# A transformer/SSD block on one core: the first 16 conditioning sums move from VectorE to TensorE

## What is computed

```python
mod = jax.nn.silu(c) @ w_ada[l] + b_ada[l]           # conditioning: 6 vectors of 1024
mod_c = jax.nn.silu(c_ctx) @ w_ada[l] + b_ada[l]     # the same for the context tokens
sh1, sc1, g1, sh2, sc2, g2 = jnp.split(mod, 6)
y, yc = hybrid_mixer(x * (1 + sc1) + sh1, ctx * (1 + csc1) + csh1, w_in[l], ..., w_out[l])
x = layer_norm(DEEPNORM_ALPHA * x + g1 * y, ln1_g[l], ln1_b[l])
x = layer_norm(DEEPNORM_ALPHA * x + g2 * swiglu(x * (1 + sc2) + sh2, ...), ln2_g[l], ln2_b[l])
```

## Time and profile before

| | |
|---|---|
| median of 3 runs | 3288.69 us (3285.17 to 3290.09) |
| profiled execution, its own time | 3289.66 us |
| its span, first to last instruction | 3287.8 us |
| mean granted TensorE clock | 0.977 |
| PE busy | 3098.7 us, 94% |
| DVE busy | 2165.9 us, 66% |
| ACT busy | 1181.9 us, 36% |
| POOL busy | 1482.7 us, 45% |
| DMA | 280.13 MB, mean 85 GB/s |

### The profile page before, as it was taken

One profiled execution on the slowest core, in us unless ns is written; L12 is line 12 of the kernel. 1 busy time (PEld: TensorE's weight loads), 2 busy tenths in 40 slices (PEclk: granted clock), 3 DMA queues, 4 the chain that ended last, 5 costly groups with the idle time before them and its releaser, 6 DMA issues. The chain is left out here.

```text
span 3287.8 us, 43629 instructions
## 1 busy us (share of the span) xinstructions
PE 3098.7 (94%) x16570; PEld 2628.7 (80%) x16570; DVE 2165.9 (66%) x3294; ACT 1181.9 (36%) x2273; POOL 1482.7 (45%) x1151
## 2 busy tenths in 40 slices
PE   4999989899999999999998999989899999999997
PEld 3798878788778888888886789878787778887886
DVE  8758977685676566635667467946776575555556
ACT  5267742361433222221113347732443322322113
POOL 0544222354434445446555464213454454555665
PEclk9999999999999999999999999999999999999999
DMA  8200042003122433425331200031022122224331
GB/s 329 97 1 1 1 144 73 15 27 128 58 77 75 148 124 124 138 86 205 125 114 45 90 1 1 1 129 33 17 87 83 66 102 77 77 94 156 97 96 64
DMA packets 96175, 280.13 MB, mean 85 GB/s; under 512 B 8416, under 2 KB 21856, under 8 KB 94560
## 3 DMA queue, kind: packets, MB, share of 16 engines
q1 hardware_dynamic: 91264, 257.42, 22.8%
q10 hardware_dynamic: 4704, 19.92, 1.5%
HBM read 224.89 MB, written 52.43 MB: 84 GB/s over the span
## 5 line engine op out<-in xcount | busy, mean ns | idle before, releaser
L3976 DVE SCALAR_TENSOR_TENSOR x_res<-ps,mod,x_res 128x512 f32<-128x512 f32 (+1 forms) x448 | 308.2, 689 | 234.8 <-PE ps L214 234.0
L3381 POOL TENSOR_TENSOR h_a_lo<-f_wraw,h_a_hi 128x512 fp32r<-128x512 f32 x126 | 183.1, 1469 | 390.7 <-ACT h_a_hi L3376 390.7
L212 PE MATMUL ps<-f_ahi,f_whi 128*128 128x512 f32 (+1 forms) x896 | 341.4, 381 | 11.2 <-DVE x_res L3976 8.4
L214 PE MATMUL ps<-f_ahi,f_wlo 128*128 128x512 f32 (+1 forms) x896 | 328.1, 366 | 0.0
L213 PE MATMUL ps<-f_alo,f_whi 128*128 128x512 f32 (+1 forms) x896 | 327.9, 366 | 0.0
L213 PE MATMUL ps<-h_lo,h_a_hi 128*128 128x512 f32 (+1 forms) x720 | 249.8, 347 | 0.0
L212 PE MATMUL ps<-h_hi,whic 128*128 128x512 f32 (+1 forms) x544 | 199.0, 366 | 15.0 <-DVE wloc L464 15.0
L212 PEld LDWEIGHTS ps<-f_ahi,f_whi 128*128 128x128 f32 x896 | 169.8, 189 | 51.7 <-DVE x_res L3976 12.3
L3732 POOL TENSOR_TENSOR f_alo<-f_gated,f_ahi 128x512 fp32r<-128x512 f32 (+1 forms) x95 | 120.1, 1281 | 180.6 <-ACT f_ahi L3922 180.5
L213 PE MATMUL ps<-h_lo,whic 128*128 128x512 f32 (+1 forms) x544 | 197.0, 362 | 0.0
L214 PE MATMUL ps<-h_hi,wloc 128*128 128x512 f32 (+1 forms) x544 | 196.7, 362 | 0.0
(11 more groups left out here) (395 smaller groups left out, 8988.1 us busy)
## 6 DMA issues: line engine op xcount, KB each, us to landing
f_wraw<-in_w_ffn SPq DMA_DIRECT2D x130, 512.0 KB, 4.5
ada_w<-in_w_ada SPq DMA_DIRECT2D x56, 512.0 KB, 6.0
h_hi_f<-in_w_ada SPq DMA_DIRECT2D x56, 512.0 KB, 4.0
o_wraw<-in_w_out SPq DMA_DIRECT2D x28, 512.0 KB, 3.6
act_spill<-f_gated SPq DMA_DIRECT2D x20, 640.0 KB, 3.3
wrawc<-in_w_in SPq DMA_DIRECT2D x24, 512.0 KB, 4.2
f_gated<-act_spill SPq DMA_DIRECT2D x19, 640.0 KB, 5.2
x_spill<-x_res ACTq DMA_DIRECT2D x16, 640.0 KB, 5.6
```

The lines of the kernel that those rows point to most:

```text
L212: pe.matmul(out, w_hi, h_hi, start=first, stop=False)
L214: return pe.matmul(out, w_lo, h_hi, start=False, stop=last)
L3381: pool.tensor_tensor(self.flat(self.lo[f]), src, raw(self.flat(self.hi[f])), ALU.subtract) \
L3976: dve.scalar_tensor_tensor(out=x, in0=pl.bank(down_bank(i) + d % 2, tn), scalar=pl.mod[:, G2 + n, who:who + 1], in1=x, op0=ALU.mult, op1=A ...
```

## The change

In the opening of layer 0 the sixteen sums are made on PE. Both condition vectors come as 16 columns (`cond_columns`, 8 KB), ACT applies Silu to them, and `tensor` multiplies each of a tile's eight 128x128 weight blocks with two columns, summed in PSUM bank 6 or 7. The weights come in that block layout (`w_first`, same size). The sums of tiles 0 and 1 stand ahead of all products in PE's queue, those of k+2 behind the products of tile k. DVE adds the bias straight from PSUM. The row-shaped conditions, still wanted for the 16 later sums, are loaded behind the last `x` tile and their Silu stands at the end of ACT's loop. Both ring blocks are loaded after `x` tile 0; DVE splits them at k = 1 in place of k = 2. The scaling by ALPHA and the stores are gone; `project_out` of layer 0 loads the input again from `xT`, and ACT scales it in five instructions, with a new count (`x_scaled`) for which DVE waits. The core of the diff:

```diff
@@ -355,34 +355,47 @@
+    columns = pl.small[:, 16:32]
+    columns_in, columns_ready = pl.sem("open_columns_in"), pl.sem("open_columns_ready")
...
     def sync(sp, ring_loads):
-        ada.start(sp)
+        sp.dma_start(columns, a["cond_columns"]).then_inc(columns_in, 16)
+        sp.sem_inc(ada.tile_done, ada.SLOTS)
+        sp.sem_inc(ada.first_done, 2 * KT)
         for n, tile in enumerate(order):
             s = n % ada.SLOTS
             sp.wait_ge(ada.tile_done, n + 1)
-            sp.dma_start(ada.w[s][:, :], a["w_ada"][0, tile]).then_inc(ada.w_in[s], 16)
+            sp.dma_start(ada.w[s][:, :], a["w_first"][tile]).then_inc(ada.w_in[s], 16)
+            if n == 0:
+                sp.dma_start(pl.bada[:, :], a["b_ada"][0]).then_inc(ada.bias_in, 16)
             if n % 2 == 1:
                 k = n // 2
                 sp.dma_start(pl.x[:, k, :], a["xT"][:, k, :]).then_inc(x_in[k], 16)
-                if k < 2:
-                    ring_loads[k]()
+                if k == 0:
+                    ring_loads[0]()
+                    ring_loads[1]()
+        sp.dma_start(ada.cond[:, :, :], a["cond"]).then_inc(ada.cond_in, 16)
         sp.dma_start(pl.const[:, :], a["consts"]).then_inc(consts_in, 16)
 
+    def tensor(pe, k):
+        if k == 0:
+            pe.wait_ge(columns_ready, 1)
+        if k >= 2:
+            pe.wait_ge(biased, k - 1)
+        sums = pl.bank(6 + k % 2, 4)
+        for j in range(2):
+            n = 2 * k + j
+            w = ada.w[n % ada.SLOTS]
+            pe.wait_ge(ada.w_in[n % ada.SLOTS], 16 * (n // ada.SLOTS + 1))
+            for i in range(KT):
+                mm = pe.matmul(sums[:, 2 * j:2 * j + 2], w[:, i * P:(i + 1) * P], columns[:, 2 * i:2 * i + 2],
+                               start=(i == 0), stop=(i == KT - 1))
+            mm.then_inc(ada.tile_done, 1)
+
     def vector(dve, between):
-        def product(n):
-            s, tile = n % ada.SLOTS, order[n]
-            dve.wait_ge(ada.w_in[s], 16 * (n // ada.SLOTS + 1))
-            dve.wait_ge(ada.tile_done, n + ada.SLOTS)
-            for c, done in ((0, ada.first_done), (1, ada.tile_done)):
-                dve.scalar_tensor_tensor(out=ada.product[:, :], in0=ada.w[s][:, :], scalar=1.0,
-                                         in1=ada.cond[:, c, :], op0=ALU.mult, op1=ALU.mult,
-                                         accum_out=pl.mod[:, tile, c:c + 1]).then_inc(done, 1)
-                if c == 0:
-                    dve.wait_ge(done, n + 1)
-
         def rest_of(k):
             dve.wait_ge(rounded, k + 1)
             dve.tensor_tensor(pl.lo[:, k, :], tmp[k % 3][:, :], raw(pl.hi[:, k, :]), ALU.subtract) \
...
-        dve.wait_ge(ada.cond_ready, 1)
         for k in range(KT):
-            product(2 * k)
-            product(2 * k + 1)
             dve.wait_ge(ada.tile_done, 2 * k + 2 + ada.SLOTS)
             part = pl.mod[:, SH1 + k:SC1 + k + 1:KT, :]
             bias = pl.bada[:, SH1 + k:SC1 + k + 1:KT].unsqueeze(2).broadcast_to([P, 2, 2])
-            dve.tensor_tensor(part, part, bias, ALU.add).then_inc(biased, 1)
+            sums = pl.bank(6 + k % 2, 4).rearrange("p (t c) -> p t c", c=2)
+            dve.tensor_tensor(part, sums, bias, ALU.add).then_inc(biased, 1)
             if k >= 1:
                 rest_of(k - 1)
-            if k == 2:
+            if k == 1:
                 between()
         rest_of(KT - 1)
         dve.wait_ge(consts_in, 16)
 
     def scalar(act, between):
-        ada.silu(act)
+        act.wait_ge(columns_in, 16)
+        act.activation(columns, columns, ACT.Silu).then_inc(columns_ready, 1)
         for k in range(KT):
             act.wait_ge(biased, k + 1)
             act.wait_ge(x_in[k], 16)
...
             act.activation(pl.hi[:, k, :], tmp[k % 3][:, :], ACT.Copy).then_inc(rounded, 1)
-            act.activation(pl.x[:, k, :], pl.x[:, k, :], ACT.Copy, scale=ALPHA).then_inc(kept, 1)
-            act.wait_ge(kept, k + 1)
-            act.dma_start(pl.x_dram[:, k, :], pl.x[:, k, :]).then_inc(spilled, 16)
             if k == 0:
                 between()
-        act.wait_ge(spilled, KT * 16)
-
-    return Lead({c: [(rest, KT)] for c in range(3)}, lambda pe: None, scalar, vector, sync=sync, tiles_in=rest,
+        ada.silu(act)
+
+    return Lead({c: [(rest, KT)] for c in range(3)}, tensor, scalar, vector, sync=sync, tiles_in=rest,
                 ada=ada)
-def multiply_along(pl, pe, ring, chunks, full, taken, tiles_in):
-
-
+def multiply_along(pl, pe, ring, chunks, full, taken, tiles_in, tile_sums):
+
+
+    tile_sums(pe, 0)
+    tile_sums(pe, 1)
     for c in ORDER:
         pe.wait_ge(taken[c], 2)
     pe.wait_ge(ring.ready, 4)
@@ -519,6 +530,8 @@
                                     pl.hi[:, k, t0:t0 + tn], pl.lo[:, k, t0:t0 + tn], k == 0, k == KT - 1)
                     if k == KT - 1:
                         mm.then_inc(full[c], 1)
+        if k + 2 < KT:
...
@@ -2309,7 +2323,8 @@
             load(0)
             load(1)
             def load_x(tiles_in, cols, signal):
-                sp.dma_start(pl.x[:, tiles_in, cols], pl.x_dram[:, tiles_in, cols]).then_inc(signal, 16)
+                source = a["xT"] if l == 0 else pl.x_dram
+                sp.dma_start(pl.x[:, tiles_in, cols], source[:, tiles_in, cols]).then_inc(signal, 16)
             load_x(slice(0, 2), slice(0, width), x_in)
             load_x(slice(6, 8), slice(0, width), x_in)
@@ -2443,6 +2458,13 @@
                     act.wait_ge(turned[p], n + 1)
                     act.activation(pl.hi[:, k, t0:t0 + tn], pl.bank(gather_bank(p, n), tn), ACT.Copy,
                                    scale=1.0 if k < 4 else gnorm(k)).then_inc(rounded[p], 1)
+                if l == 0:
+
+                    act.wait_ge(*((x_late_in, 16) if p else (x_in, 16 * (2 + len(early)))))
+                    for k0, k1, t0, t1 in ((2, 6, 512, SEQ),) if p else ((0, 2, 0, TOK), (6, 8, 0, TOK),
+                                                                         (2, 6, 0, 512), (2, 6, SEQ, TOK)):
+                        part = pl.x[:, k0:k1, t0:t1]
+                        act.activation(part, part, ACT.Copy, scale=ALPHA).then_inc(x_scaled, 1)
             act.wait_ge(next_in[0], 16)
             dve.wait_ge(x_in, 16 * (2 + len(early)))
+            if l == 0:
+                dve.wait_ge(x_scaled, 4)
             for m in range(KT):
                 if m < 4:
                     divide(tiles_of[1][m])
             dve.wait_ge(x_late_in, 16)
+            if l == 0:
+                dve.wait_ge(x_scaled, 5)
             evict(KT)
...
+        "cond_columns": f(np.stack([c[0], c_ctx], 1).reshape(KT, P, 2).transpose(1, 0, 2).reshape(P, 2 * KT)),
+        "w_first": f(blocks(w_ada[:, :, :2 * D], P)[0].reshape(2 * KT, P, D)),
```

More of the change, by code:

```diff
@@ L357, in first_inputs @@
     x_in = [pl.sem(f"open_x_in{k}") for k in range(KT)]
-    consts_in, spilled, plus_one, biased, scaled, rounded, kept, rest = (pl.sem(f"open_{x}") for x in (
-        "consts_in", "spilled", "plus_one", "biased", "scaled", "rounded", "kept", "rest"))
+    consts_in, plus_one, biased, scaled, rounded, rest = (pl.sem(f"open_{x}") for x in (
+        "consts_in", "plus_one", "biased", "scaled", "rounded", "rest"))
+    columns = pl.small[:, 16:32]
+    columns_in, columns_ready = pl.sem("open_columns_in"), pl.sem("open_columns_ready")
     def sync(sp, ring_loads):
-        ada.start(sp)
+        sp.dma_start(columns, a["cond_columns"]).then_inc(columns_in, 16)
+        sp.sem_inc(ada.tile_done, ada.SLOTS)
+        sp.sem_inc(ada.first_done, 2 * KT)
         for n, tile in enumerate(order):
@@ L521, in multiply_along @@
                         mm.then_inc(full[c], 1)
+        if k + 2 < KT:
+            tile_sums(pe, k + 2)
 def wait_full(eng, full, at, c):
@@ L632, in tensor @@
         multiply_along(self.pl, pe, self.ring, [self.chunks_of("q0"), self.chunks_of("q1")], self.full, self.taken,
-                       self.lead.tiles_in)
+                       self.lead.tiles_in, self.lead.tensor)
         self.blocks(pe)
@@ L2267, in project_out @@
     rooted, inverted, x_in, x_late_in = sem("rooted"), sem("inverted"), sem("x_in"), sem("x_late_in")
+    x_scaled = sem("x_scaled")
     normed, turned, rounded, rest = ([sem(f"{x}{p}") for p in range(2)]
```

## The result

The changed kernel took 3310.36 us, the median of 4 executions (3308.38 to 3313.17); the kernel before took 3289.39 us on the same chip, also in 4. The ratio is 1.0068, with a 95% interval of 1.0055 to 1.0082: slower by 21 us. That is outside the predicted range (3284.5 to 3300.5), on the side that the forecast named (+5.8 us) and well past its size.

The account below looks back on a forecast made before the run. DVE was taken to set the opening's pace, PE to bound the rest. Start -10.5, rounds +9.3, handover -1.0 and clock +8.0 gave +5.8 us: 3295.5 for an execution like the profiled one, 3294.5 as median; range 3284.5 to 3300.5.

Parts of the forecast that it names:

- The narrow product: PE's two-column sums in the opening: 0.107 us each, 16 a pair of tiles, 1.7 us at full clock, 3.4 at half.
- The start: Opening: PE starts the products of tile 0 at 19.1 us, where it started at 29.6, 10.5 us earlier.
- The round: Opening loop: 3.5 + 1.7 + 0.3 + 1.6 = 7.1 us at full clock, against 6.6 before; +9.3 us in all.
- The clock: Opening: PE falls to half clock behind most pauses without wide products, four to five times, costing 8.0 us.
- Spells: Stretches of PE at half clock in the opening: a little over 3.2 us long, costing 1.7 each, up to six.
- Handover: From the end of tile 7 to block 2 on PE: 3.7 us for 4.62, counted as -1.0 us.
- The sum: Start, rounds, handover and clock together: +5.8 us, with block 2 starting at 82.1.
- Behind the opening: Later sums on DVE and ACT's scalings in `project_out`: 0 us each, with bounds 0 and 2 for the scalings.
- Rival 1: Opening: the sums keep PE's clock up, 0 to 2 spells, 3286.5 to 3290 us, taken as 3287; chance 0.18.
- Rival 2: Opening: one round of products doesn't bring the clock back, +17 us, 3305; chance 0.12, plus 0.02 for a `project_out` stall.
- Rival 3: Opening: PE isn't held by DVE's order, rounds of 5.2 us, -13.6 us, 3275; chance 0.05.

Follow-up runs that it names:

- e1: The changed kernel with half of the weight blocks left out of each sum, so not all is computed: 3299.71 us, +13.6 us to the kernel before.
- e11: The changed kernel with DVE's `rest_of(k-1)` ahead of its wait for the sums of k, second run: 3308.44 us, ratio 1.0059 to the kernel before.
- e5: The changed kernel with half of the weight blocks left out and DVE's `rest_of(k-1)` ahead of its wait for the sums: 3277.93 us, ratio 0.9974.
- e6: The changed kernel with shift sums on PE, scale sums on DVE, and DVE's `rest_of(k-1)` ahead of its wait: 3279.61 us, ratio 0.9976.
- e12: The changed kernel with DVE's `rest_of(k-1)` ahead of its wait and each round's 32 narrow instructions in two groups of 16: 3296.81 us, ratio 1.0038.
- e4: The changed kernel with each of a round's 16 narrow calls behind one wide matmul, in DVE's old order: 3332.60 us, ratio 1.0140.
- e7: As e6, but with DVE's order as the change has it, `rest_of(k-1)` behind the bias add of k: 3299.87 us, ratio 1.0043.
- e8: As e5, but with the eight calls of a round one by one behind the first eight wide matmuls: 3278.09 us, ratio 0.9974.

## Why the prediction was wrong, step by step

- **The narrow product: wrong by two, and this is the step that failed.** The prediction took the earlier trace rows, 20 instructions in 2.29 us, as twenty calls, and gave the 16 calls of a pair 16 instructions. They are 32. A pair cost 3.63 us at full clock where the sum has 1.7. The duration of one instruction was nearly right: 3.63 / 32 = 0.113 us, where the row gives 2.29 / 20 = 0.114 and the prediction wrote 0.107, worth 0.1 us a pair. What was said of the bounds (1.7 to 3.4 us a pair) failed with it: they spanned the clock, not the count. The view held the answer: the loop behind that row (`query_sums`) makes one call for each 128 of 1280 tokens, ten calls, and the row says x20.
- **The start: 24.64 for 19.1.** The first two pairs take 6.96 and 6.99 us at half clock, where eight small products were expected to be a minor term. The bias of tile 1 came at 20.55 for 15.0; from there to PE's first product are 4.1 us, as predicted. The transfers were in later than the 12.5 expected: the third weight tile was noticed at 13.53, and the 3.83 MB were in at about 13.8, an estimate from 2.27 MB moved in the first 10 us and 415 GB/s after. With the right count (e1) the start is 21.86, so half of the 5.5 us is the count, and the other half the half clock and the transfers.
- **The round.** The order was read rightly: a wait between sums and products, six times, 1.65 us each (1.9 expected with its 0.3), and never between products and sums. Six rounds cost 12.5 us more by the sums than forecast (5 x 3.63 + 4.53 = 22.7 for 10.2), 1.5 less by the waits.
- **The clock.** Spells behind most pauses were expected at 8.0 us, with 1.7 for the cold start. Wide products took 5.78 us in tile 0, about 4.99 in each of tiles 1 to 5, and 8.61 for 6 and 7: 2.3 + 5 x 1.5 + 1.6 = 11.4 above 3.5 each, for 9.7. A near hit, and in part luck: four to five spells were forecast for 3.6 us without a wide product, and the changed kernel has 3.63 + 1.65 = 5.28 us without one, and six spells, shorter than the 1.7 us each of the forecast. With the forecast's own gap (e1: 1.84 + 1.65) there were four. The premise, that sums of two columns do for the clock no more than idling, fits the runs: one spell began in the middle of the sums, and in e11 each does, with no pause at all.
- **Handover:** 2.96 us for 3.7, and block 2 then runs at full clock from its first matmul (0.38 us), which before started at half.
- **The sum.** 5.5 (start) + 12.5 (sums) - 1.5 (waits) + 1.7 (clock) - 0.7 (handover) = 17.5; block 2 came at 99.49 for 82.1, which is 17.4. The forecast of +5.8 us at block 2 became +23.2, of which 21.2 reached the next stage.
- **Behind the opening** no loss shows, as predicted: the next stage starts 21.2 us later than before and the end comes 19.9 later, and differences of that size stand between two executions of one kernel. In `project_out` the view of one tile's instructions shows four scalings of 1.04 to 2.35 us, and who waits for them:

```profile
L2467 ACT ACTIVATE x_res<-x_res x4: 1037/2110/2347, 785.0 to 791.2; 128x2560 f32<-128x2560 f32 x2, 128x2048 f32<-128x2048 f32 x1, 128x1024 f32<-128x1024 f32 x1
```

They start when ACT's last rounding ahead of them is over and take 7.3 us, as forecast (7.2 to 8; ending at 767.05 to 767.85 by its own sum, not "at most" 767.5). DVE waited 6.1 us for them (to 792.3), and no matmul of PE waited for DVE's eviction.

- **The rivals.** Rival 1 (the sums keep the clock) is refuted by 33 to 35 us of the changed kernel and by e11, though 1.84 us of them did keep it in e5, e6 and e12. Rival 2 (a slow side) did not happen as worded, since each round came back to full speed, but e4 is that state, by another order. Rival 3 (PE isn't held by DVE's order) is refuted by the six waits; its 5.2 us a round are what e5 and e6 then reached. A rival with twice the instructions was missing, and there the range was too narrow. With the right count (e1) the median is 3299.71 us, at the upper end of the range; why it is 13.6 us above the kernel before, and not 5.8, is open.

Shown: the doubled count (page and timelines), the waits and their cause (e7 against e6, e1 against e5), and that the clock fell during narrow products with PE fully busy (e11; not in e12's profiled execution). Open: how long a stretch of them may be, since e12 was near its profiled time in half of its executions only, and why e4's loop never came back to full speed.

## What to carry to other kernels

Before a kind of product is priced by its neighbour in the trace, divide the instructions of that row by the calls of its loop; the ratio is a factor of the price, here two for 32-bit operands. Work of two columns an instruction on TensorE must be costed twice, by its own time and by the clock of the wide products beside it: cut it short, share it with an idle engine, or break it up with wide products. In an in-order queue, do what the bottleneck needs next ahead of a wait that it has to end itself: one line's place was worth 20 to 23 us where the other cause was cut too, and 1 to 6 where it was not.

## What the runs showed of the hardware

- A matmul call on plain 32-bit operands is two MATMUL and two weight-load instructions (256 more for 128 calls). At two columns one takes 0.113 us at full clock and 0.22 at half (6.96 / 32). The page "TensorE: Matmul & The Clock Gate" of the Trainium skill, section "Back-to-back issue gap", has about 25 ns for so few columns as the gap of a matmul by itself, and says that this is too little where each matmul loads its weights. The runs here, with new 128x128 weights for each instruction, bear that out: none came near 25 ns.
- PE busy is not PE at speed: with PE 100% busy the clock stood at 0.66 of full over ten us in e11, and at 1.00 in e12's profiled execution, by the order of the same instructions alone; the 1.84 us of each 16 sums bear out that 1.00.
- A granted clock of 1.00 in the tables needn't be one: in e4 the column reads 1.00 while 512-column matmuls start 0.85 us apart with one narrow pair between (41.73 and 42.58), and in the changed kernel it reads 1.00 while the first pairs take 6.96 us. In these stretches the spacing of the matmuls is what tells the clock; in e8 the same mix starts 0.85 us apart in the first round and 0.46 later (32.41 and 32.87).
